# Stick-breaking attention: the suffix sums as fp32r products of high and low parts, one for every later key block, in place of fp32 products with a running total

## The chip, the cores and the metric

The kernel runs on one core of a Trainium2 chip. The metric is the device time of one execution in microseconds (us), the median of several runs. TensorE is PE in the profile (its weight loads PEld), VectorE is DVE, ScalarE is ACT, GpSimd is POOL, SyncE is SP and issues every DMA.

## The reference, cut to what matters

The program is a whole two-part transformer: two layers of differential and forgetting attention, a feed-forward block, a mixer with sparse attention and stick-breaking attention, a cross attention to a memory, and a second feed-forward block. The change touches the stick-breaking attention alone, with 8 heads of width 64 and T = 512 tokens:

```python
z = jnp.einsum('bhqd,bhkd->bhqk', qb, k).astype(jnp.float32) * scale
mask = kpos[None, :] < tq[:, None]
log_rem = jnp.where(mask, jax.nn.log_sigmoid(-z), 0.0)
suffix = lax.cumsum(log_rem, axis=3, reverse=True) - log_rem
a = jnp.where(mask, jnp.exp(jax.nn.log_sigmoid(z) + suffix), 0.0)
return jnp.einsum('bhqk,bhkd->bhqd', a, v).astype(q.dtype)
```

Since log_sigmoid(-z) is -softplus(z), and log_sigmoid(z) is z - softplus(z), the weight of a key is exp(z minus the sum of softplus over this key and all later ones that the query sees).

## The kernel before, in words

Five engines run their own instruction streams in order and meet at semaphores: `on.wait_ge(*sig[key])` waits for the instruction that incremented `sig` with that key. The stick-breaking stage is written by `sb_pe`, `sb_act`, `sb_dve` and `sb_pool`. It stands after the sparse attention and before the output projection of the mixer (`wout2`, in `memory_pe`).

The work is cut into 32 blocks, listed in `SB`: for each head a (0 to 7) the four key blocks j = 3, 2, 1, 0 of 128 keys. Keys lie on the partitions and queries on the columns. Key block j sees only queries from 128*j on, so its block is n = 512 - 128*j columns wide: 128, 256, 384 and 512. Block number k has one of six PSUM banks. `C("tri")` is a 128x128 matrix with -1 where the row is at or behind the column, `C("negone")` is all -1.

What happens to a block, in order:

1. PE, `begin(k)`: scores `ps<-QS,KS` (L2002, fp32), and the mask of the diagonal `ps<-strictR,identR` (L2004, fp32r, 128 columns).
2. DVE: max(z, 0) into `SPb` (L2070), then z - 2*max(z, 0), which is -|z|, into `Ab` (L2074).
3. ACT: Exp (L2040) and Ln of 1 + x (L2042), in place in `Ab`.
4. DVE: their sum, which is softplus, into `SPb` (L2081).
5. PE: `ps<-SPb,cst` (L2013, fp32) adds minus the sum within the key block to the scores. For j < 3, `ps<-RT,cst` (L2016, fp32) adds minus the sum over all later key blocks, from the running total `RT`.
6. DVE: adds the block to the running total (L2091, or L2095 and L2096).
7. ACT: the weights, Exp out of PSUM into `Ab` (L2046).
8. PE: behind the four blocks of a head the product with the values, `ps<-Ab,VSB` (L2030, fp32, four matmuls of 512 to 128 columns, x8 in the trace: an fp32 matmul is recorded as two).

The streams are skewed over one loop counter k: DVE and ACT do steps 2 and 3 of block k, DVE step 4 of block k-1, PE step 5 of block k-2 and then `begin(k + 2)`, ACT step 7 of block k-2, and PE step 8 of a head in the round in which k-3 is its last block. Behind each odd head ACT moves two heads' output out of PSUM into `fin` (named xb in the trace, L2053) and rounds it to fp32r (`xh`, L2056), and POOL subtracts to get the low part (`xl`, L2103). ACT issues both behind Exp and Ln of the next block but one and ahead of its next Exp. Nothing else is on POOL in this stage.

A "high and low" pair is how this program writes an fp32 number as two fp32r ones: high is the value rounded to fp32r, low is what is left. All weights and most activations are split so (L342 on ACT, L350 on POOL) and multiplied with fp32r matmuls.

Of the kernel before, what the change touches and what calls it, by code (L numbers as in the profile page):

```python
# [145 lines left out]
def program(nc, wstream, xT, memT, pos, const, param, out):  # L146
# [5 lines left out]
    with ctx:  # L152
# [103 lines left out]
        Pb2 = sb("Pb2", [128, 4, L], at=nsa)  # L256
        PT2 = [sb(f"PT2{i}", [128, 640], at=nsa) for i in range(2)]
        nsa.close()
        SPb = sb("SPb", [128, 2, 4, T], at=two)
        Ab = sb("Ab", [128, 2, 4, T], at=two)  # L260
        RT = sb("RT", [128, 2, T], at=two)
        two.close()
        mid.close()
        mem = ExitStack()
# [1727 lines left out]
        def sb_psum(a, j):  # L1992
            k = SB.index((a, j))
            return PS[:, 512 * sb_bank(k):512 * sb_bank(k) + T - 128 * j]

        def sb_pe(e, on):
            def begin(k):
                a, j = SB[k]
                q0 = 128 * j
                ps = claim(on, sb_bank(k), 1, prob["sb", a, j])  # L2000
                on.wait_ge(*v_out["ks", 3])
                e.matmul(ps[:, 0:T - q0], KS[:, a // 2, q0:q0 + 128], QS[:, a, q0:T], start=True, stop=False)  # L2002
                on.wait_ge(*a_one["strict"])
                e.matmul(ps[:, 0:128], identR[:, :], strictR, start=False, stop=True).then_inc(*score("sb", a, j))  # L2004
            begin(0)
            begin(1)
            for k in range(len(SB) + 3):
                if 2 <= k < len(SB) + 2:
                    a, j = SB[k - 2]
                    u, q0 = a % 2, 128 * j  # L2010
                    n, ps = T - q0, sb_psum(a, j)
                    on.wait_ge(*v_out["sb", "sp", a, j])
                    r = e.matmul(ps, C("tri"), SPb[:, u, j, 0:n], start=False, stop=True, skip_group_check=True)  # L2013
                    if j < 3:
                        on.wait_ge(*v_out["sb", "rt", a, j + 1])
                        r = e.matmul(ps[:, 128:n], C("negone"), RT[:, u, q0 + 128:T], start=False, stop=True,  # L2016
                                     skip_group_check=True)
                    r.then_inc(*one_mm("suffix", a, j))
                if k + 2 < len(SB):
                    begin(k + 2)  # L2020
                if k >= 3 and SB[k - 3][1] == 0:
                    a = SB[k - 3][0]
                    u, t_ = a % 2, a // 2
                    if u == 0:
                        claim(on, 6 + t_ % 2, 1, a_out["sb", "out", t_])
                    o = PS[:, 512 * (6 + t_ % 2):512 * (7 + t_ % 2)]
                    on.wait_ge(*prob["sb", a, 0])
                    for j in range(4):
                        vt = VSB[:, j, t_, 2 * u:2 * u + 2, :]
                        r = e.matmul(o[:, 128 * j:T], vt.rearrange("p a b -> p (a b)"), Ab[:, u, j, 0:T - 128 * j],  # L2030
                                     start=u == 0 and j == 0, stop=u == 1 and j == 3)
                    r.then_inc(*pv("sb", a))

        def sb_act(e, on):
            for k in range(len(SB) + 3):
                if k < len(SB):
                    a, j = SB[k]
                    e_ = Ab[:, a % 2, j, 0:T - 128 * j]
                    on.wait_ge(*v_out["sb", "arg", a, j])
                    e.activation(e_, e_, ACT.Exp).then_inc(*a_out("sb", "exp", a, j))  # L2040
                    on.wait_ge(*a_out["sb", "exp", a, j])
                    e.activation(e_, e_, ACT.Ln, bias=1.0).then_inc(*a_out("sb", "ln", a, j))  # L2042
                if 2 <= k < len(SB) + 2:
                    a, j = SB[k - 2]
                    on.wait_ge(*one_mm["suffix", a, j])
                    e.activation(Ab[:, a % 2, j, 0:T - 128 * j], sb_psum(a, j), ACT.Exp).then_inc(*prob("sb", a, j))  # L2046
                if k >= 3 and SB[k - 3][1] == 0 and SB[k - 3][0] % 2:
                    a = SB[k - 3][0]
                    t_ = a // 2
                    f, before = place(("sb", t_))  # L2050
                    on.wait_ge(*pv["sb", a])
                    on.wait_ge(*x_lo[("ao",) + before])
                    e.activation(fin[:, f, 0:T], PS[:, 512 * (6 + t_ % 2):512 * (7 + t_ % 2)], ACT.Copy).then_inc(  # L2053
                        *a_out("sb", "out", t_))
                    on.wait_ge(*a_out.now())
                    e.activation(xh[:, 4 + t_, M:L], fin[:, f, 0:T], ACT.Copy).then_inc(*x_hi("ao", "sb", t_))  # L2056

        def sb_dve(e, on):
            for k in range(len(SB) + 3):
                if k < len(SB):  # L2060
                    a, j = SB[k]
                    u, n = a % 2, T - 128 * j
                    o, sp = sb_psum(a, j), SPb[:, u, j, 0:n]
                    on.wait_ge(*score["sb", a, j])
                    if k == 0:
                        on.wait_ge(*turn["nsa1", 3])
                        on.wait_ge(*v_end["nsa1", 3, "gate"])
                    if a >= 2:
                        on.wait_ge(*one_mm["suffix", a - 2, 0])
                    e.tensor_scalar(sp, o, 0.0, None, ALU.max, ALU.bypass).then_inc(*v_out("sb", "max", a, j))  # L2070
                    on.wait_ge(*v_out.now())
                    if a >= 2:
# [3 lines left out]
                if 1 <= k < len(SB) + 1:  # L2076
                    a, j = SB[k - 1]
                    u, n = a % 2, T - 128 * j
                    sp = SPb[:, u, j, 0:n]
                    on.wait_ge(*a_out["sb", "ln", a, j])  # L2080
                    e.tensor_tensor(sp, sp, Ab[:, u, j, 0:n], ALU.add).then_inc(*v_out("sb", "sp", a, j))  # L2081
                if 2 <= k < len(SB) + 2:
                    a, j = SB[k - 2]
                    u, q0 = a % 2, 128 * j
                    n = T - q0
                    sp = SPb[:, u, j, 0:n]
                    on.wait_ge(*v_out["sb", "sp", a, j])
                    if j == 3:
                        if a >= 2:
                            on.wait_ge(*one_mm["suffix", a - 2, 0])  # L2090
                        e.tensor_copy(RT[:, u, 384:512], sp).then_inc(*v_out("sb", "rt", a, 3))  # L2091
                    elif j:
                        on.wait_ge(*one_mm["suffix", a, j])
                        on.wait_ge(*v_out["sb", "rt", a, j + 1])
                        e.tensor_copy(RT[:, u, q0:q0 + 128], sp[:, 0:128])  # L2095
                        e.tensor_tensor(RT[:, u, q0 + 128:T], RT[:, u, q0 + 128:T], sp[:, 128:n], ALU.add).then_inc(  # L2096
                            *v_out("sb", "rt", a, j))

        def sb_pool(e, on):
            for t_ in range(4):  # L2100
                f, _ = place(("sb", t_))
                on.wait_ge(*x_hi["ao", "sb", t_])
                e.tensor_tensor(xl[:, 4 + t_, M:L], fin[:, f, 0:T], xh[:, 4 + t_, M:L].bitcast(F32),  # L2103
                                ALU.subtract).then_inc(*x_lo("ao", "sb", t_))


        def mix_ao(k):
# [475 lines left out]
```

## Time and profile before

| | |
|---|---|
| median of 3 runs | 1977.92 us (1977.88 to 1987.02) |
| the profiled execution | 1985.47 us |
| its span | 1983.7 us |
| PE busy | 1921.9 us, 97% |
| PEld / DVE / ACT / POOL busy | 83% / 39% / 36% / 36% |
| chain that ended last, by engine | PE 88%, DVE 6%, ACT 3% |

The span is the stretch between the first and the last instruction in the trace. Busy shares are averages over stages with different limits. The chain that ended last is followed back from the last instruction, at each step to what released it.

### The profile page before, as it was taken

The numbers are of one execution on the slowest core, as the hardware profiler recorded it, in microseconds if no ns is written. First come the engines' busy times: TensorE is split into PE (matmuls) and PEld (weight loads), VectorE is DVE, ScalarE is ACT, GpSimd is POOL, SyncE is SP. The second block draws the span as 40 slices with busy tenths as digits, with TensorE's granted clock in tenths as the row PEclk, the third lists the DMA queues.
The fourth block names the chain that finished last, engine by engine and source line by source line (L and its number), as shares of the span: only waits on it lengthen the run. The fifth ranks groups of instructions, "written<-read, shape, count | busy, mean of one in ns | idle before, by whom it ended". The sixth has DMA issues, their size and how long they took to land.

```text
span 1983.7 us, 26722 instructions
## 1 busy us (share of the span) xinstructions
PE 1921.9 (97%) x10968; PEld 1646.1 (83%) x10968; DVE 779.8 (39%) x1308; ACT 707.4 (36%) x1328; POOL 712.1 (36%) x343
## 2 busy tenths in 40 slices
PE   7999989999998999999999999899999999999999
PEld 6999878989987897888888878799867878888887
DVE  5433373464326536441112255536676451111001
ACT  3112355321125544223222223435565552222211
POOL 4333201353331014555554423320003435555443
PEclk9999899999999999999999999979999999999999
DMA  4222200122221003222223233110002212222223
GB/s 142 86 79 82 65 1 1 54 85 86 78 85 41 1 13 100 87 94 96 96 91 98 92 109 118 65 43 2 1 1 97 95 54 96 96 96 96 91 88 108
DMA packets 40585, 144.22 MB, mean 73 GB/s; under 512 B 4624, under 2 KB 4880, under 8 KB 40336
## 3 DMA queue, kind: packets, MB, share of 16 engines
q1 hardware_dynamic: 40464, 142.51, 21.6%
q8 instruction: 87, 1.43, 0.3%
q14 instruction: 34, 0.28, 0.0%
HBM read 140.40 MB, written 2.10 MB: 72 GB/s over the span
## 4 chain that ended last, share of the span: by engine, by line
PE 88%; DVE 6%; ACT 3%; issue 1%; DMA 1%; POOL 0%; SPq 0%; DVEq 0%; ACTq 0%
PE ps L354 22%; PE ps L355 22%; PE ps L356 22%; PE ps L871 6%; PE ps L852 5%; PE ps L861 3%; PE ps L2030 1%; DMA raw<-wstream 1%; PE ps L2013 1%; DVE xl L425 1%; PE ps L2002 1%; PE ps L500 1%; PE ps L989 1%; ACT wh L342 1%; PE ps L1774 1%
## 5 line engine op out<-in xcount | busy, mean ns | idle before, releaser
L350 POOL TENSOR_TENSOR wl<-raw,wh 128x1024 fp32r<-128x1024 f32 (+2 forms) x254 | 603.6, 2376 | 838.9 <-ACT wh L342 838.9
L354 PE MATMUL ps<-xh,wh 128*128 128x512 f32 (+3 forms) x1752 | 626.4, 358 | 20.3 <-POOL wl L350 12.5
L355 PE MATMUL ps<-xl,wh 128*128 128x512 f32 (+3 forms) x1752 | 619.9, 354 | 0.0
L356 PE MATMUL ps<-xh,wl 128*128 128x512 f32 (+3 forms) x1752 | 618.1, 353 | 0.0
L342 ACT ACTIVATE wh<-raw 128x1024 fp32r<-128x1024 f32 (+2 forms) x254 | 266.0, 1047 | 969.8 <-PE ps L356 903.1
L354 PEld LDWEIGHTS ps<-xh,wh 128*128 128x128 f32 x1752 | 330.8, 189 | 75.4 <-issue 18.4
L355 PEld LDWEIGHTS ps<-xl,wh 128*128 128x128 f32 x1752 | 331.1, 189 | 49.0 <-issue 1.7
L356 PEld LDWEIGHTS ps<-xh,wl 128*128 128x128 f32 x1752 | 331.5, 189 | 47.2
L1116 POOL TENSOR_TENSOR xl<-xb,xh 128x512 fp32r<-128x512 f32 (+1 forms) x22 | 26.1, 1186 | 339.9 <-ACT xh L1025 339.9
L355 PE MATMUL ps<-aL,wh 128*128 128x512 f32 x352 | 139.4, 396 | 0.0
L356 PE MATMUL ps<-aH,wl 128*128 128x512 f32 x352 | 139.2, 396 | 0.0
L354 PE MATMUL ps<-aH,wh 128*128 128x512 f32 x352 | 139.2, 395 | 0.0
L910 DVE TENSOR_REDUCE nm<-ps 128x1 f32<-128x144 f32 (+7 forms) x208 | 99.6, 490 | 79.2 <-PE ps L852 78.6
L1409 DVE TENSOR_TENSOR tmpn<-xb,ps 128x512 f32<-128x512 f32 x44 | 30.3, 688 | 211.3 <-PE ps L356 208.6
L354 PE MATMUL ps<-wh,xh 128*128 128x256 f32 (+1 forms) x352 | 101.7, 289 | 5.8 <-DVE xb L1522 3.7
L897 ACT ACTIVATE PT<-ps 128x256 f32<-128x256 f32 (+4 forms) x142 | 70.6, 497 | 85.2 <-PE ps L861 79.7
L355 PE MATMUL ps<-wl,xh 128*128 128x256 f32 (+1 forms) x352 | 100.8, 286 | 0.0
L356 PE MATMUL ps<-wh,xl 128*128 128x256 f32 (+1 forms) x352 | 100.7, 286 | 0.0
L889 ACT ACTIVATE Pb<-ps,nm 128x256 f32<-128x256 f32 (+7 forms) x144 | 75.1, 523 | 31.4 <-DVE nm L910 30.6
L354 PEld LDWEIGHTS ps<-aH,wh 128*128 128x128 f32 x352 | 66.2, 188 | 16.1
L355 PEld LDWEIGHTS ps<-aL,wh 128*128 128x128 f32 x352 | 66.2, 188 | 16.0
L356 PEld LDWEIGHTS ps<-aH,wl 128*128 128x128 f32 x352 | 66.1, 188 | 15.9
(346 smaller groups left out, 2666.4 us busy)
## 6 DMA issues: line engine op xcount, KB each, us to landing
raw<-wstream SPq DMA_DIRECT2D x236, 512.0 KB, 3.5
raw<-wstream SPq DMA_DIRECT2D x16, 384.0 KB, 3.0
raw<-wstream SPq DMA_DIRECT2D x10, 528.0 KB, 3.6
h<-xT SPq DMA_DIRECT2D x4, 528.0 KB, 6.6
out<-h SPq DMA_DIRECT2D x8, 256.0 KB, 3.9
hm<-memT SPq DMA_DIRECT2D x1, 1024.0 KB, 4.8
cst<-const SPq DMA_DIRECT2D x1, 720.5 KB, 9.5
cst<-const SPq DMA_DIRECT2D x1, 320.0 KB, 4.0
```

What stands on the lines that cost most here:

```text
L342: e.activation(wh[p % 2][:, 0:n], raw[c % 2][:, 0:n], ACT.Copy).then_inc(*w_hi(p))
L350: e.tensor_tensor(wl[p % 2][:, 0:n], raw[c % 2][:, 0:n], wh[p % 2][:, 0:n].bitcast(F32), ALU.subtract).then_inc(*w_lo(p))
L354: e.matmul(o, w_h, x_h, start=start, stop=False)
L355: e.matmul(o, w_h, x_l, start=False, stop=False)
L356: return e.matmul(o, w_l, x_h, start=False, stop=stop)
L852: r = e.matmul(ps[:, x.o0 + lo:x.o0 + hi], lhsT, rhs, start=start, stop=stop)
L861: r = e.transpose(ps[0:b - a, 128 * j:128 * j + 128], plan.source(u)[:, a:b], ident)
L871: r = e.matmul(PS[:, lo + x.cols[0]:lo + x.cols[1]], buf[0:b - a, 128 * j:128 * j + 128], x.value(j, b - a), start=j == 0, stop=j == len(x ...
L889: e.activation(plan.slot(s)[:, 0:x.n], PS[:, lo:lo + x.n], ACT.Exp, bias=nm[:, s % 8:s % 8 + 1], accum_out=x.total[0]).then_inc(*prob(name ...
L897: e.activation(plan.PT[i % 2][:, 0:n], PS[:, lo:lo + n], ACT.Copy).then_inc(*a_flip(name, u))
L910: e.tensor_reduce(nm[:, u % 8:u % 8 + 1], PS[:, lo:lo + x.n], AX.X, ALU.max, negate=True).then_inc(*peak(name, u))
L1409: e.tensor_tensor(tmpn[:, f % 2, 0:T], xb[:, f % 2, 0:T], PS[:, 512 * b + 512:512 * b + 1024], ALU.mult).then_inc(*v_out(st, "gated", f))
```

## The change

The running total `RT` and its three DVE instructions (L2091, L2095, L2096 of before) go away, and so do both fp32 products of step 5. In their place each block's softplus, now kept in `Ab`, is rounded to fp32r into `SPh` (ACT for j = 3 and 2, a DVE cast for j = 1 and 0), and POOL subtracts to get the low part `SPl`. PE multiplies both parts with `negR` for every later key block of the head (0, 1, 2 or 3 of them), and with `triR` for the block itself. `SPb` shrinks to two buffers that hold max(z, 0) only. POOL's output subtractions are put between its new ones: behind the low part of block j = 2 of heads 2, 4 and 6, and one at the end. Two small ACT instructions make `triR` and `negR` at the start of the stage.

```diff
         def sb_pe(e, on):
...
-                    on.wait_ge(*v_out["sb", "sp", a, j])
-                    r = e.matmul(ps, C("tri"), SPb[:, u, j, 0:n], start=False, stop=True, skip_group_check=True)
-                    if j < 3:
-                        on.wait_ge(*v_out["sb", "rt", a, j + 1])
-                        r = e.matmul(ps[:, 128:n], C("negone"), RT[:, u, q0 + 128:T], start=False, stop=True,
+                    on.wait_ge(*a_one["tri"])
+                    for i in range(3, j, -1):
+                        for part in (SPh, SPl):
+                            e.matmul(ps[:, 128 * (i - j):n], negR, part[:, u, i, 0:T - 128 * i], start=False, stop=True,
                                      skip_group_check=True)
+                    for part, done in ((SPh, sb_high(a, j)), (SPl, x_lo["sb", "sp", a, j])):
+                        on.wait_ge(*done)
+                        r = e.matmul(ps, triR, part[:, u, j, 0:n], start=False, stop=True, skip_group_check=True)
                     r.then_inc(*one_mm("suffix", a, j))
...
         def sb_act(e, on):
+            e.activation(triR, C("tri"), ACT.Copy)
+            e.activation(negR, C("negone"), ACT.Copy).then_inc(*a_one("tri"))
...
+                if 1 <= k < len(SB) + 1 and SB[k - 1][1] > 1:
+                    a, j = SB[k - 1]
+                    on.wait_ge(*v_out["sb", "sp", a, j])
+                    sb_low_free(on, a, j)
+                    e.activation(SPh[:, a % 2, j, 0:T - 128 * j], Ab[:, a % 2, j, 0:T - 128 * j], ACT.Copy).then_inc(
+                        *x_hi("sb", "high", a, j))
...
         def sb_dve(e, on):
...
-                    sp = SPb[:, u, j, 0:n]
+                    t = Ab[:, u, j, 0:n]
                     on.wait_ge(*a_out["sb", "ln", a, j])
-                    e.tensor_tensor(sp, sp, Ab[:, u, j, 0:n], ALU.add).then_inc(*v_out("sb", "sp", a, j))
-                if 2 <= k < len(SB) + 2:
...
-                        e.tensor_copy(RT[:, u, q0:q0 + 128], sp[:, 0:128])
-                        e.tensor_tensor(RT[:, u, q0 + 128:T], RT[:, u, q0 + 128:T], sp[:, 128:n], ALU.add).then_inc(
-                            *v_out("sb", "rt", a, j))
+                    e.tensor_tensor(t, SPb[:, (k - 1) % 2, 0:n], t, ALU.add).then_inc(*v_out("sb", "sp", a, j))
+                    if j <= 1:
+                        on.wait_ge(*v_out.now())
+                        sb_low_free(on, a, j)
+                        e.tensor_copy(SPh[:, u, j, 0:n], t).then_inc(*v_out("sb", "high", a, j))
 
         def sb_pool(e, on):
...
+            for k, (a, j) in enumerate(SB):
+                u, n = a % 2, T - 128 * j
+                sb_low_free(on, a, j)
+                on.wait_ge(*sb_high(a, j))
+                e.tensor_tensor(SPl[:, u, j, 0:n], Ab[:, u, j, 0:n], SPh[:, u, j, 0:n].bitcast(F32),
+                                ALU.subtract).then_inc(*x_lo("sb", "sp", a, j))
+                if j == 2 and a in (2, 4, 6):
+                    outputs(a // 2 - 1)
+            outputs(3)
```

Three places show how the instructions stand. The first is PE in a head's last round, before: the sums of block j = 0, the scores of a block of the next head, and the sums of that head's block j = 3.

```order
L2013 MATMUL ps<-SPb,cst 128x512
L2016 MATMUL ps<-RT,cst 128x384
L2002 MATMUL ps<-QS,KS 128x512
L2004 MATMUL ps<-strictR,identR 128x128
L2013 MATMUL ps<-SPb,cst 128x128
L2002 MATMUL ps<-QS,KS 128x128
```

The same place after the change:

```order
L2026 MATMUL ps<-SPh,negR 128x128
L2026 MATMUL ps<-SPl,negR 128x128
L2026 MATMUL ps<-SPh,negR 128x256
L2026 MATMUL ps<-SPl,negR 128x256
L2026 MATMUL ps<-SPh,negR 128x384
L2026 MATMUL ps<-SPl,negR 128x384
L2030 MATMUL ps<-SPh,triR 128x512
L2030 MATMUL ps<-SPl,triR 128x512
L2013 MATMUL ps<-QS,KS 128x512
L2015 MATMUL ps<-strictR,identR 128x128
L2030 MATMUL ps<-SPh,triR 128x128
L2030 MATMUL ps<-SPl,triR 128x128
```

L2026 are the products with `negR`, L2030 those with `triR`; each fp32 product over a running total has become up to six fp32r ones of 128, 256 and 384 columns, and only the last `triR` product needs the newest low part.

The second place is DVE, over two rounds in which a new head begins, before:

```order
L2081 TENSOR_TENSOR SPb<-SPb,Ab 128x384
L2095 COPY RT<-SPb 128x128
L2096 TENSOR_TENSOR RT<-RT,SPb 128x128
L2070 TENSOR_SCALAR SPb<-ps 128x128
L2074 SCALAR_TENSOR_TENSOR Ab<-SPb,ps 128x128
L2081 TENSOR_TENSOR SPb<-SPb,Ab 128x512
L2095 COPY RT<-SPb 128x128
```

and after, from the same point on (the sum of the previous head's block j = 1 is the first row of each):

```order
L2102 TENSOR_TENSOR Ab<-SPb,Ab 128x384
L2106 CAST SPh<-Ab 128x384
L2091 TENSOR_SCALAR SPb<-ps 128x128
L2095 SCALAR_TENSOR_TENSOR Ab<-SPb,ps 128x128
L2102 TENSOR_TENSOR Ab<-SPb,Ab 128x512
L2106 CAST SPh<-Ab 128x512
L2091 TENSOR_SCALAR SPb<-ps 128x256
```

L2102 is the softplus sum, now with both inputs and the output in SBUF as before; the running total's two instructions behind it are gone, and a cast (L2106) of the same width stands there.

The third place is POOL, before: the splits of the mixer's last weights, the low parts of the sparse attention's output, the four low parts of this stage's output, and the splits for the output projection.

```order
L350 TENSOR_TENSOR wl<-raw,wh 128x1056 x6
L350 TENSOR_TENSOR wl<-raw,wh 128x1024 x6
L1116 TENSOR_TENSOR xl<-xb,xh 128x4x128 x4
L2103 TENSOR_TENSOR xl<-xb,xh 128x512 x4
L350 TENSOR_TENSOR wl<-raw,wh 128x1024 x14
L1116 TENSOR_TENSOR aml<-xb,amh 128x2x128 x4
```

and after, in the middle of the stage (the end of head 1, head 2 and its successor):

```order
L2118 TENSOR_TENSOR SPl<-Ab,SPh 128x512
L2118 TENSOR_TENSOR SPl<-Ab,SPh 128x128
L2118 TENSOR_TENSOR SPl<-Ab,SPh 128x256
L2112 TENSOR_TENSOR xl<-xb,xh 128x512
L2118 TENSOR_TENSOR SPl<-Ab,SPh 128x384
L2118 TENSOR_TENSOR SPl<-Ab,SPh 128x512
L2118 TENSOR_TENSOR SPl<-Ab,SPh 128x128
```

The output's low part (L2112) now stands between the low parts of two blocks (L2118) of one head, and what comes behind it on POOL waits for it.

## Rows read from the trace of the kernel before

**Rows 1.** Windows view: us, busy PE, PEld, DVE, ACT, POOL, granted clock, DMA
```profile
...
1320.00:1335.00 15.00, 15.00 (x78) 15.00 (x77) 6.71 (x25) 6.17 (x27) 0.00 (x0) 0.50 0.00 0
...
1428.00:1497.00 69.00, 66.93 (x266) 43.51 (x265) 51.36 (x137) 44.67 (x103) 5.08 (x4) 0.99 0.00 1
...
```

**Rows 2.** Chain of waits in order of time, the stick-breaking stage: start, us, what
```profile
...
1447.29 2.22 PE ps L2030 x8
...
1449.53 0.61 ACT xb L2053
...
1450.16 0.63 ACT xh L2056
1450.79 0.53 ACT Ab L2040
...
1451.34 0.64 ACT Ab L2042
...
1452.00 0.70 DVE SPb L2081
...
1452.75 1.13 PE ps L2013 x2
...
1456.00 2.21 PE ps L2030 x8
...
1464.22 2.22 PE ps L2030 x8
...
1498.40 0.23 PE ps L354
...
```

**Rows 3.** Chain of waits from 1456.00 to 1464.22 (8.22 us), by line
```profile
...
by line: PE ps L2030 32.7%; PE ps L2013 28.2%; PE ps L2002 26.3%; PE ps L2016 15.8%; PE ps L2004 2.9%
...
```

**Rows 4.** Groups of instructions, 1428 to 1497
```profile
...
L2081 DVE TENSOR_TENSOR SPb<-SPb,Ab 128x128 f32<-128x128 f32 (+3 forms) x32 | 15.7, 491 | 2.6 <-ACT Ab L2042 2.6
L2074 DVE SCALAR_TENSOR_TENSOR Ab<-SPb,ps 128x128 f32<-128x128 f32 (+3 forms) x32 | 15.6, 487 | 1.1
L2070 DVE TENSOR_SCALAR SPb<-ps 128x128 f32<-128x128 f32 (+3 forms) x32 | 15.5, 486 | 0.6 <-PE ps L2004 0.2
...
```

**Rows 5.** Timeline of PE: fp32r matmuls of 264 columns, back to back
```profile
...
1290.02 0.28 PE L354 MATMUL ps<-wh,xh 128*128 128x264 f32 x1
1290.14 0.28 PE L355 MATMUL ps<-wl,xh 128*128 128x264 f32 x1
...
```

**Rows 6.** Timeline of PE in the sparse attention: 128 and 64 columns
```profile
...
1395.89 0.61 PE L861 MATMUL ps<-identR,Pb 128*128 128x128 f32 x4
1396.25 0.70 PE L852 MATMUL ps<-KSW,QN 128*128 128x512 f32 x2
1396.79 0.22 PE L852 MATMUL ps<-maskR,identR 128*128 128x128 f32 x1
1396.85 1.05 PE L871 MATMUL ps<-VSW,PT 128*128 128x64 f32 x8
1397.73 0.50 PE L861 MATMUL ps<-identR,Pb 128*128 128x128 f32 x3
```

**Rows 7.** Groups by form, POOL
```profile
...
L2103 POOL TENSOR_TENSOR xl<-xb,xh 128x512 fp32r<-128x512 f32 x4 | 5.1, 1276 | 65.6 <-ACT xh L2056 65.6
...
L1116 POOL TENSOR_TENSOR aml<-xb,amh 128x256 fp32r<-128x256 f32 x4 | 2.9, 728 | 16.2 <-ACT amh L1025 16.2
...
```

**Rows 8.** Groups by form, DVE copies from SBUF to SBUF
```profile
...
L2236 DVE COPY QM<-xb 64x512 f32<-64x512 f32 x4 | 1.7, 421 | 0.1
...
L2226 DVE COPY KM<-xb 128x256 f32<-128x256 f32 x2 | 0.6, 294 | 0.1
...
```

**Rows 9.** Timeline, 444 to 448: POOL and DVE side by side
```profile
...
444.12 2.40 POOL L350 TENSOR_TENSOR wl<-raw,wh 128x1024 fp32r<-128x1024 f32 x1 [3.61 <-ACT wh L342]
...
444.35 2.72 DVE L513 TENSOR_TENSOR scratch<-xb,cst 128x512 f32<-128x512 f32 x1
...
447.10 0.69 DVE L515 TENSOR_TENSOR scratch<-ps,cst 128x512 f32<-128x512 f32 x1
...
```

More of the change, by code:

```diff
@@ L258, in program @@
         nsa.close()
-        SPb = sb("SPb", [128, 2, 4, T], at=two)
+        SPb = sb("SPb", [128, 2, T], at=two)
         Ab = sb("Ab", [128, 2, 4, T], at=two)
-        RT = sb("RT", [128, 2, T], at=two)
+        SPh = sb("SPh", [128, 2, 4, T], F32R, at=two)
+        SPl = sb("SPl", [128, 2, 4, T], F32R, at=two)
+        triR, negR = (sb(n, [128, 128], F32R, at=two)[:, :] for n in ("triR", "negR"))
         two.close()
@@ L1994, in sb_psum, with sb_high, sb_low_free @@
             return PS[:, 512 * sb_bank(k):512 * sb_bank(k) + T - 128 * j]
+        def sb_high(a, j):
+            return (x_hi if j > 1 else v_out)["sb", "high", a, j]
+        def sb_low_free(on, a, j):
+            if a >= 2:
+                on.wait_ge(*one_mm["suffix", a - 2, 0])
         def sb_pe(e, on):
@@ L2062, in sb_dve @@
                     u, n = a % 2, T - 128 * j
-                    o, sp = sb_psum(a, j), SPb[:, u, j, 0:n]
+                    o, sp = sb_psum(a, j), SPb[:, k % 2, 0:n]
                     on.wait_ge(*score["sb", a, j])
@@ L2078, in sb_dve, with outputs @@
                     u, n = a % 2, T - 128 * j
-                    sp = SPb[:, u, j, 0:n]
+                    t = Ab[:, u, j, 0:n]
                     on.wait_ge(*a_out["sb", "ln", a, j])
-                    e.tensor_tensor(sp, sp, Ab[:, u, j, 0:n], ALU.add).then_inc(*v_out("sb", "sp", a, j))
-                if 2 <= k < len(SB) + 2:
[L2083 to L2094, printed above, removed]
-                        e.tensor_copy(RT[:, u, q0:q0 + 128], sp[:, 0:128])
-                        e.tensor_tensor(RT[:, u, q0 + 128:T], RT[:, u, q0 + 128:T], sp[:, 128:n], ALU.add).then_inc(
-                            *v_out("sb", "rt", a, j))
+                    e.tensor_tensor(t, SPb[:, (k - 1) % 2, 0:n], t, ALU.add).then_inc(*v_out("sb", "sp", a, j))
[3 more added lines that the diff above has]
+                        e.tensor_copy(SPh[:, u, j, 0:n], t).then_inc(*v_out("sb", "high", a, j))
         def sb_pool(e, on):
-            for t_ in range(4):
+            def outputs(t_):
                 f, _ = place(("sb", t_))
```

4 lines of the change are left out of this document (2 added, 2 removed).

## The prediction

> **What bounds the kernel now.** I read the windows view of the stage first. From 1428 to 1497 PE is busy 66.93 of 69.00 us, at a granted clock of 0.99; DVE has 51.36, ACT 44.67 and POOL 5.08 [rows 1]. So PE paces the stage, and POOL is nearly free. The chain of waits tells how evenly. The product with the values (L2030) begins at 1447.29, 1456.00 and 1464.22 [rows 2]. A head therefore takes 8.71 us or 8.22 us in turn, 16.93 us for two. The 8.22 us are PE work without a gap: the chain by line names PE alone [rows 3]. The 8.71 us hold a detour: L2030 ends, ACT moves the output out (L2053) and rounds it (L2056), only then does Exp and Ln of the next head's 512-column block (L2040, L2042), DVE adds (L2081), and PE, which has meanwhile run out of other work, begins L2013 at 1452.75 [rows 2]. The reader is to keep this detour in mind: the change puts two more instructions behind its last step.
>
> **What the change removes on PE.** In the head of 8.22 us, L2013 has 28.2% and L2016 15.8% [rows 3], which is 2.32 + 1.30 = 3.62 us a head.
>
> **What it adds on PE.** 20 fp32r matmuls a head: two of 512 columns, four of 384, six of 256, eight of 128. 512 columns take 0.23 (L354 at 1498.40) [rows 2]; 264 columns take 0.12 back to back [rows 5], which I use for 256; 384 lies between, 0.18. For 128 columns the trace gives two ends. The fp32r mask product takes 0.06 (1396.79 to 1396.85), with its weights loaded under a longer matmul. Eight of only 64 columns take 0.88, 0.11 each, and there the loads must set the pace. Four of 128 columns in a row take 0.36, 0.09 each [rows 6]. The new ones also come in rows, so I take 0.09. Sum: 0.46 + 0.72 + 0.72 + 0.72 = 2.62 us (2.4 to 2.8). PE saves 1.0 us a head (0.8 to 1.2), and its own work falls from 8.22 to 7.2. If nothing else came in, the stage would lose 8 us.
>
> **What it adds beside PE.** DVE loses the running total and gains casts of 384 and 512 columns. I price them as copies in SBUF: 421 ns for 512 columns, 294 for 256, so about 0.36 for 384 [rows 8]. ACT gains two roundings of the narrow blocks a head, each under the 0.63 of the 512-column one (L2056 to L2040) [rows 2], so its 44.67 us of 69 [rows 1] stay under 55. POOL gains one subtraction a block: 1276 ns for 512 columns and 728 for 256 give 2.14 ns a column, so 1.00 for 384 and 0.45 for 128 [rows 7]; 3.46 us a head, 28 us in all, where it did almost nothing. By busy time it all fits. By latency it doesn't: before, PE could begin a block's own sum as soon as DVE had added (L2081); now a cast (0.42) and a subtraction (1.28) come between, for the widest block.
>
> **DVE and POOL get in each other's way.** At 444.12 POOL begins a subtraction of 2.40 us. DVE begins at 444.35 a tensor_tensor with both inputs in SBUF and takes 2.72 us, where the one at 447.10 with an input in PSUM takes 0.69 [rows 9]. The first ends 0.55 us after POOL's end (447.07 against 446.52). So a DVE addition of two SBUF tensors waits for a POOL subtraction that runs. L2081 is such an addition, and POOL now subtracts in this stage. L2070 and L2074 read PSUM and pass.
> The Trainium skill ("SBUF — State Buffer", Who interferes with whom) has this as a rule: with two SBUF inputs against a GpSimd instruction that reads SBUF, the second one to issue is blocked until the first finishes. Read literally, the blocked addition would cost its full 0.69 behind POOL's end and not the 0.55 of the row; with five blocked ones in two heads that would be 0.14 x 5 x 4 = 2.8 us more than my sum. The row has a duration, so I use the row.
>
> **The even head (a new pair begins), walked through.** From one L2030 to the next: L2030 and hand-over 2.24; ACT move 0.63 and rounding 0.63 (1449.53 to 1450.79) [rows 2]; POOL's low part of the output 1.28, which now stands ahead of the low part of block j = 1, 1.00 [rows 7]; DVE's sum of block j = 0, which arrives while that runs and ends 0.55 behind it [rows 9]; cast 0.42 [rows 8]; low part 1.28 [rows 7]; then PE's last triR product 0.23, the scores of the next block but one and its mask 0.86 + 0.06, two 128-column products 0.18, and a narrow score and mask 0.28: 1.61. (0.86 is four passes' worth of 512 fp32 columns, as in L2030, whose 512, 384, 256 and 128 columns take 2.21 together [rows 2]: 2.21 x 512/1280 = 0.88.) Sum: 2.24 + 1.26 + 2.28 + 0.55 + 0.42 + 1.28 + 1.61 = 9.64, and four hand-overs of 0.02 to 0.05 more: 9.8 us, against 8.71.
>
> **The odd head.** PE needs 7.2. DVE: L2070, L2074 and L2081 have 15.5 + 15.6 + 15.7 = 46.8 us for 8 heads [rows 4], 5.85 a head, with the casts 6.6. On top L2081 waits: the 1.28 of the low part of block j = 0 runs while DVE does its two operations on the next 256 columns (0.84), 0.44 too long; the 1.00 of block j = 1 against two on 128 columns (0.57), 0.43; the 0.73 of block j = 2, which starts late since ACT rounds it, about 0.4. Together 7.9; neighbouring DVE operations overlap a little, so I take 7.8, against 8.22. In the odd head DVE takes PE's place as the bound, and 0.4 of the 1.0 us saved is left.
>
> **The ends.** The first and the last head have no other head's work to cover the longer way. Behind the last sum stood fp32 products of 512 and 384 columns (at the 2.21 us for 1280 columns of L2030, 0.88 + 0.66); now cast and subtraction 1.70 and one product of 0.23: 0.4 more, and one or two port waits of 0.4: 1.2 at either end. The two ACT instructions for `triR` and `negR` lie where ACT waits for the sparse attention's last output: nothing; without that cover at most 2 x 0.63.
>
> **Sum.** A pair: 9.8 + 7.8 = 17.6 against 16.93, +0.7; four pairs +2.7; ends +2.4. Together +5 us on the profiled execution (1985.47 to about 1990.5). The rest of the program isn't touched. The three runs before lie at 1977.88, 1977.92 and 1987.02, so the profiled one is of the upper kind; on the median I forecast 1977.9 + 5 = 1983. A difference under 0.5% (9.9 us) can hardly be told from no change here, given that spread.
>
> **Rivals.**
> *PE's saving comes through* (10%). Speaks for it: PE is the bound today, and POOL's subtractions could hide in the three rounds between a block's scores and its sums. Against it: the detour already costs 0.49 us where nothing was added behind it. Time: 1977.9 - 8 = 1970; with 0.06 for each 128-column matmul 1968, which is just 0.5%.
> *The ports don't clash here* (15%): POOL's short subtractions slip in beside DVE's PSUM work. Then the odd head falls to PE's 7.2 and the even one still has the added cast and subtraction, less 0.5: 9.3. A pair is 16.5, the ends cost 0.8: -1.7 + 1.6, no change, 1978.
> *Slower by over 0.5%* (14%): TensorE is granted the lower of its two levels. From 1320 to 1335 the clock is 0.50 (1.2 GHz) with PE busy throughout, on 78 matmuls [rows 1]. The change makes this stage one of narrow matmuls with gaps. At half rate PE's 14.4 us of work in a pair of 17.6 becomes 28.8, so a low stretch of L us costs 0.39 L. It decides from 13 us on; 15 us as in the row cost 6, on top of the 5: 1989.
> *POOL waits for DVE as DVE does for POOL* (10%): the trace shows one direction only [rows 9]. Six POOL instructions of a pair are on the walked way (three in each head); if each meets half of a DVE sum (0.49) [rows 4], that is 0.25 x 6 x 4 = 6 us more: 1989, at the bound.
> *My forecast* (51%): 1979 to 1987 as its own range.
>
> **Numbers.** The range must take in the case without clashes and most of the slow one: 1974 to 1992, which leaves out the saving that comes through and a long low stretch. Faster by over 0.5%: 4%, only the far end of the first rival. Slower: 18%, over half of the two rivals at 1989 and a tail of my own case. The rest, 78%, within 0.5%.
>
> **What the profile would show.** Starts of the value product 7.8 and 9.8 us apart in turn. PE waiting for POOL's low parts in the waits view, above all before triR products of 512 columns, some 0.5 us each. The sum of DVE (L2102) at a mean well above 0.49, since it waits for the port. Fp32r 128-column products 0.09 apart. Wrong if POOL isn't in the chain, if the mean of DVE's sum stays at 491 ns, or if the clock in the stage falls below 0.95.

## The result, and the profile after

The changed kernel takes 1985.18 us (median of 22 runs, 1981.69 to 1994.07) against 1978.87 us for the kernel before on the same chip. The ratio is 1.0027, with an interval of 1.0016 to 1.0038: 5.3 us slower (the medians lie 6.3 apart), inside the half per cent. Two runs of before, at 3154 and 6661 us, are of a slower state and stay out of the ratio.

| | before | after |
|---|---|---|
| span of the profiled execution | 1983.7 us | 1987.3 us |
| PE busy | 1921.9 us | 1914.4 us |
| DVE / ACT / POOL busy | 779.8 / 707.4 / 712.1 us | 789.1 / 711.7 / 741.5 us |
| first score load to the start of the last value matmul | 1427.2 to 1498.1: 70.9 us | 1423.2 to 1501.7: 78.5 us |

The two spans should not be subtracted as they stand. The profiled execution of before has a stretch at half clock in the sparse attention (0.50 from 1320 to 1335 [rows 1]); that of after has 1.00 there. The stage itself can be compared. It is 7.6 us longer in this execution.

The chain of waits after the change, two heads of it (start, us, what), answers to [rows 2] and [rows 3]:

```profile
...
1458.10 0.17 PE ps L2026 x2
1458.28 0.29 PE ps L2030 x2
...
1459.06 0.51 PE ps L2026 x4
1459.57 0.35 PE ps L2030 x2
...
1460.62 0.86 PE ps L2026 x6
1461.49 0.46 PE ps L2030 x2
...
1462.87 0.23 PE ps L2030 x2
...
1463.42 2.22 PE ps L2043 x8
...
1465.67 0.61 ACT xb L2074
...
1466.30 0.64 ACT xh L2077
...
1467.01 1.27 POOL xl L2112
1468.28 1.42 POOL SPl L2118
...
1469.74 0.44 PE ps L2030
...
1473.69 2.21 PE ps L2043 x8
...
```

L2043 is the value product, once L2030. The odd head runs from 1455.89 to 1463.42 in 7.53 us on PE alone. Its lines L2026 (negR) and L2030 (triR) are the 20 new matmuls: 0.17 + 0.29 + 0.51 + 0.35 + 0.86 + 0.46 + 0.23 = 2.87 us, where 3.62 stood. The even head takes 10.27 us, from 1463.42 to 1473.69. It runs over the output's move (L2074) and rounding (L2077) to POOL: the output's low part (L2112), the low part of block j = 1 (L2118), and at 1469.74 back to PE. From there to the next value product, 3.95 us, PE works without another wait.

The waits view of the stage says the same from the side of PE, and shows what POOL waits for:

```profile
...
POOL SPl L2118 <- ACT SPh L2062: 20.1, 13, 3.2
...
PEld ps L2030 <- POOL SPl L2118: 11.8, 9, 2.7
...
POOL SPl L2118 <- DVE SPh L2106: 11.1, 13, 1.1
PE ps L2030 <- POOL SPl L2118: 9.0, 6, 2.5
...
```

PE and its weight loads wait for POOL's low parts, up to 2.7 us at a time. The three long waits of PE, 2.47 to 2.48 us each, are all before the `triR` product of block j = 1 (384 columns) in heads 2, 4 and 6; the one wait before a product of 512 columns is 0.85 us, in head 7. The groups of the stage (mean ns behind the busy time) answer to [rows 4]:

```profile
...
L2118 POOL TENSOR_TENSOR SPl<-Ab,SPh 128x256 fp32r<-128x256 f32 (+3 forms) x31 | 28.7, 924 | 32.6 <-ACT SPh L2062 20.1 <-DVE SPh L2106 11.1 <-PE ps L2030 1.3
L2102 DVE TENSOR_TENSOR Ab<-SPb,Ab 128x384 f32<-128x384 f32 (+3 forms) x30 | 22.8, 761 | 6.0 <-ACT Ab L2057 6.0
...
L2106 DVE CAST SPh<-Ab 128x384 fp32r<-128x384 f32 (+1 forms) x16 | 8.3, 520 | 0.5
...
```

L2102 is the addition that had a mean of 491 ns as L2081 [rows 4]; it does the same work and now has 761. The cast has 520 ns. The timeline inside the even head's gap shows both directions of the waiting:

```profile
...
1467.01 1.27 POOL L2112 TENSOR_TENSOR xl<-xb,xh 128x512 fp32r<-128x512 f32 x1 [2.13 <-ACT xh L2077]
...
1468.14 0.69 DVE L2102 TENSOR_TENSOR Ab<-SPb,Ab 128x512 f32<-128x512 f32 x1 [1.93 <-ACT Ab L2057]
1468.23 1.46 POOL L2118 TENSOR_TENSOR SPl<-Ab,SPh 128x384 fp32r<-128x384 f32 x1
...
1468.87 1.10 DVE L2106 CAST SPh<-Ab 128x512 fp32r<-128x512 f32 x1
...
1469.74 0.44 PE L2030 MATMUL ps<-SPl,triR 128*128 128x384 f32 x1 [2.48 <-POOL SPl L2118]
...
1470.05 1.28 POOL L2118 TENSOR_TENSOR SPl<-Ab,SPh 128x512 fp32r<-128x512 f32 x1 [0.36 <-DVE SPh L2106]
...
1471.83 0.39 PE L2030 MATMUL ps<-SPl,triR 128*128 128x512 f32 x1
...
```

DVE's addition begins at 1468.14. POOL's subtraction of 384 columns begins 0.09 later and takes 1.46 us, where 1.01 is its usual time. DVE's cast begins at 1468.87, meets that subtraction and takes 1.10, where 0.43 is usual. The low part of block j = 0 is ready at 1471.33, half a microsecond before its product (1471.83).

The last view is the windows of the stage, with the columns of [rows 1]:

```profile
...
1445.00:1450.00 5.00, 2.88 (x18) 2.28 (x16) 3.10 (x7) 3.16 (x7) 3.01 (x3) 1.00 0.00 0
1450.00:1455.00 5.00, 4.66 (x15) 3.63 (x15) 3.48 (x7) 2.21 (x6) 2.02 (x3) 0.66 0.00 0
1465.00:1470.00 5.00, 2.52 (x17) 2.16 (x17) 2.97 (x7) 3.15 (x7) 2.68 (x2) 1.00 0.00 0
1485.00:1490.00 5.00, 2.53 (x11) 2.17 (x11) 3.82 (x7) 3.21 (x9) 3.96 (x4) 0.86 0.00 0
1490.00:1495.00 5.00, 5.00 (x19) 3.26 (x18) 3.09 (x6) 2.92 (x7) 1.05 (x3) 0.80 0.00 0
1428.00:1497.00 69.00, 60.01 (x296) 45.19 (x295) 56.48 (x104) 46.55 (x112) 31.07 (x33) 0.95 0.00 1
...
```

The granted clock is 0.66 behind the gap at 1445 to 1450, and 0.86 and 0.80 around that of 1485 to 1495. Behind the equal gap of 1465 to 1470 it stays at 1.00. Over the stage (1428 to 1497) it is 0.95, where before had 0.99 [rows 1].

The timed runs are recorded with their mean granted clock too. Its mean is 0.9914 over the 22 runs of the changed kernel, and 0.9931 to 0.9934 over those of the kernel before in the three sessions of experiments below (without one run of 3156 us). Between the changed kernel's own runs, 1981.69 us at 0.995 and 1994.07 at 0.985, a thousandth of clock goes with about 1.2 us. So about 2 of the 5.3 us are the clock's; this is an estimate, across sessions.

### The profile page after: what moved, and what is told of

Same layout as the page of the kernel before. It is cut to its first block, busy times and chain, and to the rows that moved or that the text cites. A ratio compares the mean times of both kernels' runs of the same rounds, so it can differ in the third digit from the quotient of the medians.

```text
span 1987.3 us, 26867 instructions
## 1 busy us (share of the span) xinstructions
PE 1914.4 (96%) x11016; PEld 1643.1 (83%) x11016; DVE 789.1 (40%) x1284; ACT 711.7 (36%) x1346; POOL 741.5 (37%) x375
## 4 chain that ended last, share of the span: by engine, by line
PE 86%; DVE 7%; ACT 3%; DMA 1%; issue 1%; POOL 1%; SPq 0%; DVEq 0%; ACTq 0%
PE ps L356 22%; PE ps L357 22%; PE ps L358 22%; PE ps L873 5%; PE ps L854 5%; PE ps L863 3%; DMA raw<-wstream 1%; ACT wh L344 1%; PE ps L2043 1%; DVE xl L427 1%; PE ps L502 1%; PE ps L991 1%; POOL wl L352 1%; PE ps L2013 1%; PE ps L410 0%
## 5 line engine op out<-in xcount | busy, mean ns | idle before, releaser
L899 ACT ACTIVATE PT<-ps 128x256 f32<-128x256 f32 (+4 forms) x142 | 70.6, 497 | 79.7 <-PE ps L863 74.6
```

Of the source, the lines that this page charges most:

```text
L899: e.activation(plan.PT[i % 2][:, 0:n], PS[:, lo:lo + n], ACT.Copy).then_inc(*a_flip(name, u))
```

## The experiments

All are timed in 5 rounds against the kernel before on the same chip; the ratio is to that kernel. This table gives the time from one value product's start to the next in each profiled execution, by the timeline. Heads 1, 3 and 5 are odd, 2, 4 and 6 even. The stage is counted from the first score load to the start of the last value matmul. The last row's kernel was timed twice.

| kernel | ratio (interval) | heads 1, 3, 5 | heads 2, 4, 6 | head 7 | stage |
|---|---|---|---|---|---|
| before | 1 | 8.22, 8.22, 8.22 | 8.72, 8.71, 8.43 | 6.56 | 70.9 |
| changed | 1.0027 (1.0016 to 1.0038) | 7.90, 7.53, 7.56 | 11.86, 10.27, 11.53 | 6.96 | 78.5 |
| outputs behind j = 0 | 1.0030 (1.0015 to 1.0046) | 7.92, 7.52, 7.54 | 9.64, 9.65, 9.30 | 7.21 | 73.7 |
| outputs in POOL's gap | 1.0036 (1.0024 to 1.0048) | 7.89, 8.50, 8.50 | 9.26, 9.25, 8.92 | 8.39 | 77.7 |
| POOL writes only | 1.0005 (0.9988 to 1.0022) | 7.53, 7.52, 7.53 | 9.80, 9.80, 9.46 | 6.47 | 72.3 |
| no low parts | 0.9977 (0.9961 to 0.9993) | 7.53, 7.53, 7.53 | 8.59, 8.59, 8.55 | 5.63 | 67.4 |
| own blocks in fp32 | 1.0019 (1.0004 to 1.0035) | 8.42, 8.41, 8.42 | 9.73, 9.73, 9.44 | 6.43 | 74.6 |
| filler in the gap | 1.0018 (1.0008 to 1.0029) | 7.89, 7.57, 7.56 | 10.28, 10.28, 9.93 | 7.27 | 75.7 |
| output later | 1.0027 (1.0013 to 1.0041) | 7.89, 8.47, 8.47 | 7.90, 7.89, 7.56 | 8.43 | 73.7 |
| output later, POOL writes only | 0.9976 (0.9966 to 0.9986) | 7.53, 7.52, 7.52 | 7.53, 7.53, 7.20 | 6.47 | 65.4 |
| before, output later | 1.0004 (0.9994 to 1.0014) | 8.23, 8.24, 8.25 | 8.67, 8.68, 8.67 | 6.63 | 70.9 |
| block j = 0 in fp32, output early | 1.0009 (0.9993 to 1.0025) | 7.92, 7.92, 7.92 | 8.82, 8.81, 8.48 | 6.63 | 71.7 |
| block j = 0 in fp32, output later | 0.9991 (0.9982 to 0.9999), 0.9989 (0.9980 to 0.9998) | 7.92, 7.92, 7.92 | 7.92, 7.92, 7.58 | 6.48 | 68.6 |

**The outputs behind block j = 0.**

```diff
-                if j == 2 and a in (2, 4, 6):
+                if j == 0 and a in (2, 4, 6):
                     outputs(a // 2 - 1)
```

> The changed kernel, with POOL's low part of the output moved from between the low parts of blocks j = 2 and j = 1 of heads 2, 4 and 6 to behind that of block j = 0. Theory (in the even head the whole chain runs through POOL: output 1.27, then the low parts): each of the three even heads loses that 1.27, PE waits about 3.8 us less in all, 1981.5 us. Rival (the even head waits for DVE's sums or for the clock, POOL's place in it is by chance): within 1 us of the changed kernel, 1985.

Half of it came. The even heads fell from 10.27 to 9.64, not by 1.27, and the ratio, 1.0030, can't be told from the changed kernel's. The chain, and two rows of PE's timeline, say why:

```profile
...
1464.17 0.44 DVE SPh L2106
...
1464.68 1.27 POOL SPl L2118
1465.95 0.58 POOL xl L2112
1466.54 0.66 issue
1467.20 0.47 POOL SPl L2118
...
1467.71 0.33 PE ps L2030
...
1468.37 2.21 PE ps L2043 x8
...
```

```profile
...
1466.01 0.50 PE L2030 MATMUL ps<-SPl,triR 128*128 128x512 f32 x1 [0.86 <-POOL SPl L2118]
...
1467.71 0.33 PE L2030 MATMUL ps<-SPl,triR 128*128 128x128 f32 x1 [0.17 <-POOL SPl L2118]
...
```

With the output's low part out of the way, the path over ACT's Exp and Ln, DVE's sum and cast and the low part of block j = 0 is the long one. PE waits 0.86 us for that low part, and 0.17 for the next head's block j = 3, before which the output's low part now stands; the single wait of 2.48 us is gone. So POOL's place in the chain is shown, and a second path of nearly the same length stands behind it. In this profiled execution the stage is 2.8 us longer than before, in the medians the kernel is 5.2 us slower; the mean clock of its runs, 0.9912 against 0.9931, would account for about 2 of the difference.

**No low parts.** POOL's 32 subtractions are left out and PE multiplies the high part twice, so the sums lack the low parts.

```diff
-                        for part in (SPh, SPl):
+                        for part in (SPh, SPh):
...
-                    for part, done in ((SPh, sb_high(a, j)), (SPl, x_lo["sb", "sp", a, j])):
+                    for part, done in ((SPh, sb_high(a, j)), (SPh, sb_high(a, j))):
```

> The changed kernel without POOL's subtractions: PE multiplies the high part twice in their place, so the sums lose their low parts, and PE has the same 20 fp32r products a head. Theory (PE's saving is real and is lost behind POOL): PE is the bound again, value products 7.3 to 7.5 us apart, 1971 to 1972 us, 7 under the kernel before. Rival (128-column fp32r products in rows save nothing over fp32 ones): about 1979, as before.

PE's saving is real: odd heads of 7.53 us, and 0.9977, some 4.5 us where 7 was expected. The rival is out. But the even heads take 8.59, not 7.5: their chain runs over the output's move and rounding, Exp, Ln, DVE's sum and cast, and on to the rounding on ACT of the next head's block j = 3. POOL costs at most the rest of 10.27.

**POOL writes only.** Each subtraction is a memset of equal length, which reads nothing; the low parts are left out as above.

```diff
-                e.tensor_tensor(SPl[:, u, j, 0:n], Ab[:, u, j, 0:n], SPh[:, u, j, 0:n].bitcast(F32),
-                                ALU.subtract).then_inc(*x_lo("sb", "sp", a, j))
+                if k >= 2:
+                    on.wait_ge(*x_lo[("sb", "sp") + SB[k - 2]])
+                flat = SPl[:, k % 2, :, :].rearrange("p a b -> p (a b)")
+                e.memset(flat[:, 0:{128: 429, 256: 754, 384: 1077, 512: 1402}[n]].bitcast(F32), 0.0).then_inc(
+                    *x_lo("sb", "sp", a, j))
```

> The changed kernel with each subtraction of POOL replaced by a fill of the low-part buffer that is sized to take as long (0.455, 0.73, 1.0, 1.27 us) and reads nothing; PE multiplies the high part twice, so the low parts are left out. It keeps POOL's latency and takes away the meeting of two readers. Theory with the port as a term of its own: L2102's mean falls from 761 ns to about 490, odd heads fall to 7.3 us, even ones to about 9, total 1979 to 1980. Rival (only the latency of cast and subtraction matters, the port nothing): 1985.

The groups of its stage:

```profile
...
L2121 POOL MEMSET SPl<- 128x1402 f32 (+3 forms) x29 | 25.4, 877 | 24.5 <-ACT SPh L2062 13.1 <-DVE SPh L2106 7.4 <-issue 4.0
...
L2102 DVE TENSOR_TENSOR Ab<-SPb,Ab 128x256 f32<-128x256 f32 (+3 forms) x27 | 13.3, 493 | 6.8 <-ACT Ab L2057 6.8
...
```

And DVE's cast beside one of the fills, in an even head:

```profile
...
1442.41 1.00 POOL L2121 MEMSET SPl<- 128x1077 f32 x1
...
1443.06 0.63 DVE L2106 CAST SPh<-Ab 128x512 fp32r<-128x512 f32 x1
...
```

POOL's instructions have a mean of 877 ns, near the 924 of the changed kernel's subtractions, and DVE's addition is back at 493 ns. The stage loses 6.2 us of 78.5, of which some 3 are the clock (below). The port is a term of its own. The total is the expected one, the heads are not: the even ones are still at 9.80, 0.47 under 10.27, which is what POOL's subtraction of 384 columns had lost behind DVE's addition. The rest is latency: the output's move and rounding, its low part and the low part of j = 1. The fills do not free the cast: in the three even heads it starts while a fill runs and takes 0.62 to 0.63 us for 0.43.

**Own blocks in fp32.** The product with `tri` is done in fp32 on `Ab`, as before; the pairs serve later key blocks only, and block j = 0 isn't split.

```diff
+                    if j < 3:
+                        on.wait_ge(*x_lo["sb", "sp", a, j + 1])
...
-                        r = e.matmul(ps, triR, part[:, u, j, 0:n], start=False, stop=True, skip_group_check=True)
+                    on.wait_ge(*v_out["sb", "sp", a, j])
+                    r = e.matmul(ps, C("tri"), Ab[:, u, j, 0:n], start=False, stop=True, skip_group_check=True)
...
```

> The changed kernel with the sum within a key block done in fp32 from the softplus itself, as before; only the products for later key blocks use the high and low parts, which nobody needs before the next block, and block j = 0 isn't split at all. PE's work a head: 8.2 less 1.30 of the running-total products plus 1.4 for the 12 fp32r ones, 8.3. Theory (the cost is the split in the way of the own block): about the time before, 1978 to 1981. Rival (POOL's and DVE's load on the ports slows the stage wherever the split stands): 1984 or more.

1.0019 (1981.83 us against 1977.63), a little over the theory's range. The odd heads, 8.41, are PE work and dearer than before (8.22): the twelve products for later blocks cost more than the three over a running total. The even ones stay at 9.73, since the output still stands ahead of the low part of j = 1, which block j = 0 needs.

**The outputs in POOL's gap**, behind the low part of block j = 3 of heads 3, 5 and 7.

> The changed kernel, with POOL's low part of the output behind the low part of block j = 3 of heads 3, 5 and 7, where POOL next waits 1.8 to 3.2 us for a rounding. Theory (with the outputs behind block j = 0 they stood in the way again, ahead of the low part of the next head's block j = 3, and PE still waited): even heads fall from 9.64 there to 9.0 or less, ratio to the kernel before 1.001 to 1.002. Rival (the even head is held by the chain of ACT and DVE behind the output's move and rounding, not by POOL): as with the outputs behind j = 0, 1.003.

Not as expected: 1.0036. The even heads fell to 9.25, but the odd ones rose to 8.50, so a pair took 17.75 against 17.80, and against 17.17 with the outputs behind j = 0. The even head's chain runs over ACT's Exp and Ln of the 512-column block and then over DVE, as the rival said; then DVE's addition of 256 columns stands beside the output's subtraction (1.27 us from 1448.32) and takes 1.34 us for 0.42, and DVE stays the chain into the odd head. So the place is worth 0.6 us a pair, and no place of these three is free. The end of the stage ran at clocks of 0.64 and 0.68, and head 7 took 8.39.

**The output later**: in addition ACT's move and rounding come one round later, behind Exp and Ln of the next 512-column block.

```diff
-                if k >= 3 and SB[k - 3][1] == 0 and SB[k - 3][0] % 2:
-                    a = SB[k - 3][0]
+                if k >= 4 and SB[k - 4][1] == 0 and SB[k - 4][0] % 2:
+                    a = SB[k - 4][0]
```

> The same, and ACT moves and rounds the output one round later, behind Exp and Ln of the 512-column block and not ahead of them. Theory (the detour over the output is what the low parts lengthen): even heads fall to about 7.6 to 8.0, PE is the bound in most heads, and PE's saving shows: ratio 0.997 to 0.9985, 1972 to 1975. Rival (POOL's and DVE's waits for each other hold every head): 1.000 to 1.002.

The even heads did what was expected (7.90), the ratio did not: 1.0027. Its profiled execution had a low stretch in the sparse attention, so the stage counts: 73.7 us, 2.8 more than before. Heads 1 to 6 together are 2.3 us shorter than before; the start is 1.2 longer, head 7 1.9, and the last value product, at a clock of 0.55 from 1500 on, takes 4.6 us for 2.4. The chain from 1450 to 1475, by line, and the group of DVE's addition:

```profile
...
by line: DVE Ab L2102 44.3%; DVE SPb L2091 22.9%; DVE Ab L2095 17.8%; issue 11.6%; DVE SPh L2106 7.1%; DVEq L142 0.5%
...
```

```profile
...
L2102 DVE TENSOR_TENSOR Ab<-SPb,Ab 128x128 f32<-128x128 f32 (+3 forms) x32 | 27.5, 859 | 0.5 <-ACT Ab L2057 0.5
...
```

DVE alone is the bound, at 7.9 us a head and 8.47 where POOL's output falls in, and its additions take 859 ns each. So the rival names the right cause in the middle heads, though 1.0027 is over its range too, and the next run tests it.

**The output later, POOL writes only.**

> The kernel with the later output, whose chain of waits is DVE alone (7.89 and 8.47 us a head), with POOL's subtractions replaced by fills of equal length that read nothing; PE multiplies the high part twice, so the low parts are left out. Theory (DVE is the bound there only because its sums wait for POOL's reads): both heads fall to PE's 7.5, the mean of L2102 to 0.49, ratio 0.996 to 0.997. Rival (DVE is too slow without POOL too): 7.8 or more a head.

```profile
...
L2102 DVE TENSOR_TENSOR Ab<-SPb,Ab 128x256 f32<-128x256 f32 (+3 forms) x27 | 13.3, 493 | 1.6 <-ACT Ab L2057 1.6
...
```

Heads 1 to 5 fall to PE's 7.53, the addition to 493 ns, the ratio to 0.9976, a little over the expected 0.996 to 0.997. DVE's own work isn't the bound; its waits for POOL's reads are. 859 - 493 = 0.37 us for each of four additions a head.

**The kernel before, output later.** The same edit of ACT on the kernel before.

> The kernel before, with the same later place of the output's move and rounding on ACT, nothing else. Theory: the 0.49 us of the three even heads go, 1.5 us, ratio 0.9992; the rest of the kernel before is PE work. If it were 0.997 or less, the later place alone and not PE's saving would explain what the previous kernel gains.

Not as expected: 0.9992 lies just outside the interval around 1.0004, and the even heads stay at 8.67. Their chain has another link now, and the timeline shows what stood beside it:

```profile
...
1438.87 0.45 PE ps L2016 x2
...
1439.34 1.34 DVE RT L2095
1440.68 0.34 DVE RT L2096
...
1441.07 0.91 PE ps L2016 x2
...
```

```profile
...
1437.72 0.23 DVE L2095 COPY RT<-SPb 128x128 f32<-128x128 f32 x1 [1.54 <-PE ps L2016]
...
1439.33 1.27 POOL L2103 TENSOR_TENSOR xl<-xb,xh 128x512 fp32r<-128x512 f32 x1 [21.33 <-ACT xh L2056]
1439.34 1.34 DVE L2095 COPY RT<-SPb 128x128 f32<-128x128 f32 x1
...
```

The copy of 128 columns into the running total (L2095) takes 1.34 us and holds PE back. Elsewhere it takes 0.23, also where DVE has first waited 1.54 us for PE's product over the total. It takes 1.34 three times, once in each even head, and each time POOL's subtraction for the output (L2103, 1.27 us) began 0.01 us before it; the copy ends 0.08 us behind POOL's end. In its new place the output's subtraction meets this copy. So the detour over the output is gone here, and a wait of DVE for POOL has come in its stead. That the even heads would fall to the odd ones' 8.24 without it is likely, but no run shows it.

**Block j = 0 in fp32, output later, and output early.** Block j = 0 has no later key block, so its pair serves only its own sum. Here that sum is an fp32 product, and the widest cast and subtraction go.

```diff
+                    if j == 0:
+                        on.wait_ge(*v_out["sb", "sp", a, 0])
+                        r = e.matmul(ps, C("tri"), Ab[:, u, 0, 0:n], start=False, stop=True, skip_group_check=True)
-                    for part, done in ((SPh, sb_high(a, j)), (SPl, x_lo["sb", "sp", a, j])):
+                    for part, done in ((SPh, sb_high(a, j)), (SPl, x_lo["sb", "sp", a, j])) if j else ():
```

> As the kernel with the later output, but the own sum of block j = 0 is done in fp32 from the softplus itself, so the 512-column cast and subtraction, which no later block needs, go. PE's work a head 7.5 + 0.4 = 7.9. Theory: no POOL or DVE step of 512 columns is left in the way, the ends of the stage lose their extra 1.2 us each, ratio 0.997 to 0.998. Rival (PE's work alone counts): slower than the kernel with the later output by 0.4 x 8 = 3 us.

> The kernel with the own sum of block j = 0 in fp32, with ACT's move and rounding of the output back ahead of Exp and Ln. Theory: the detour ends in DVE's sum as in the kernel before, and the even heads take 8.4 to 8.7 us against 7.92; ratio 1.0000 to 1.0005. Rival (the fp32 own sum alone makes the gain): ratio 0.999, as with the later output.

> The kernel with the own sum of block j = 0 in fp32 and the later output once more, beside the other three. Expected 0.9985 to 0.9995, heads of 7.92 us.

With the output later the kernel is faster than the kernel before: 0.9991 and 0.9989 in two sessions, some 2 us, with intervals that end at 0.9999 and 0.9998. Less than the expected 0.997 to 0.998, since the stage, 68.6 us against 70.9, had no more than 2.3 us to give. One head from value product to value product, by line of the chain:

```profile
...
by line: PE ps L2046 27.9%; PE ps L2013 27.9%; PE ps L2026 19.6%; PE ps L2033 10.8%; PE ps L2030 10.8%; PE ps L2015 3.8%
...
```

Nothing but PE is left in it, at 7.92 us, the 7.5 + 0.4 of the expectation. With the output early the even heads take 8.8 and the gain is gone (1.0009, an interval across 1). The intervals of the two kernels overlap a little; that the place of the output matters is shown by the heads.

**Filler in the gap.** Two fp32 products that nobody reads, put before PE's wait for the low part of j = 1 of heads 2, 4 and 6.

```diff
+                        if j == 1 and a in (2, 4, 6) and part is SPl:
+                            on.wait_ge(*a_out["sb", "out", a // 2 - 1])
+                            b = 6 + (a // 2 - 1) % 2
+                            for _ in range(2):
+                                e.matmul(PS[:, 512 * b:512 * b + 512], KS[:, 0, 0:128], QS[:, 0, :], start=True, stop=True,
+                                         skip_group_check=True)
                         on.wait_ge(*done)
```

> The changed kernel, with two fp32 products of 512 columns (1.7 us) into the unused output bank in the 2.4 us for which PE waits for the low part of block j = 1 of heads 2, 4 and 6; nobody reads them. Theory (in the profile of the changed kernel the granted clock fell to 0.66 and 0.80 after two of these gaps, and these even heads took 11.9 and 11.5 us where the one at full clock took 10.27): all even heads take about 10.3, ratio 1.001 to 1.002. Rival (the falls are rare in other executions and don't bear on the median): ratio 1.0027 as without them.

The even heads take 10.28, 10.28 and 9.93 and the granted clock stays at 1.00 in the stage from 1425 on. Against 11.86, 10.27 and 11.53 that is 3.2 us in the profiled execution. The ratio is 1.0018, under 1.0027, but the two intervals overlap. The mean clock of its runs is 0.9940 against 0.9914 for the changed kernel, and none of them is under 0.992. That agrees with some 2 us of the median for the clock.

## Why the prediction was right, point by point

**The size.** 1983 was forecast, 5 us over the median then known; 5.3 us by the ratio was measured. In part that is luck. The sum takes four pairs, but only three even heads (2, 4 and 6) stand behind an output: three at +1.09 and four odd ones at -0.42 are +1.6, not +2.7, and with the ends 4.0. At full clock the profiled stage is 4.4 us longer, with even heads dearer and odd heads cheaper than forecast, and the clock, which is in no term, brought more.

**PE's work.** The new matmuls cost 2.87 us a head, not 2.62. Two of 128 columns take 0.17 once a head and 0.22 to 0.23 otherwise, where 0.18 was priced; two of 256 take 0.29, not 0.24. 384 and 512 columns were priced right. PE's floor is 7.53, not 7.2.

**The even head.** Forecast 9.8, measured 10.27 at full clock. The links up to PE's restart were named rightly: move, rounding, output's low part, low part of j = 1. In the step "DVE's sum of block j = 0, which arrives while that runs and ends 0.55 behind it" the order was wrong: the sum began 0.09 before POOL's subtraction of j = 1, and POOL waited, 1.46 for 1.00. That is the rival in which POOL waits for DVE too, with its price at one of six places. Behind that the forecast's path was wrong: it goes on over DVE's sum, the cast and the low part of j = 0, 0.55 + 0.42 + 1.28 and then 1.61 on PE, 3.86 us. In the trace PE restarts at 1469.74, works 3.95 us on its own and doesn't wait for that low part. That the two are almost equally long is luck. For the same reason the sign "above all before triR products of 512 columns, some 0.5 us each" failed: the waits are 2.5 us before those of 384 columns. In the run with the outputs behind j = 0 the sum, the cast and that low part are in the chain.

**The odd head.** Forecast 7.8 with DVE as the bound, measured 7.53 to 7.56 with PE as the bound. The step "in the odd head DVE takes PE's place" failed for heads 3 and 5: in the 2.5 us that PE loses in an even head DVE catches up. Head 1, which has no such gap ahead of it, takes 7.90 on a chain of DVE up to 1440.64, as forecast. Its own pace was sized well: with the output later, when PE no longer idles, the heads without POOL's output take 7.89 on a chain of DVE.

**The ends.** From the first score load to the first value product 12.8 us against 11.7: 1.1 more, forecast 1.2. At head 7 only 0.4 more, forecast 1.2.

**The port.** That DVE's addition waits for POOL's reads was read from one place [rows 9] and holds: 491 to 761 ns, and 493 with a POOL that only writes. The two operations on PSUM pass, as forecast (the row for it, at 447.10, stood where POOL was idle and couldn't show it): 692 and 687 ns for 512 columns (L2091, L2095) against 687 and 688 before. The step prices the waits of the addition alone; the casts wait as well, 1.10 for 0.43 in each of the three even heads, and their mean is 520 ns where 0.36 and 0.42 were priced. The Trainium skill ("SBUF — State Buffer", Who interferes with whom) gives the same condition, two SBUF inputs against a GpSimd instruction that reads, and for the addition the memset run agrees with it. Its words let the blocked instruction follow the first in full; the rows give less, 0.55 us behind POOL's end for a 0.69 us addition, and, for POOL behind DVE's end at 1468.83, 0.86 us of a 1.00 us subtraction.

**The clock.** It was priced as a rival at 14% and left out of the sum. Over the stage it stood at 0.95, just at the forecast's own sign of being wrong. In the profiled execution it fell twice for a short time at PE's gaps and made two even heads 1.6 us longer each (11.86 against 10.27, and head 6 11.53 against the 9.93 of the filler's run).

In the stage of that execution: three even heads at full clock 1.5 to 1.6 more each (4.6), odd heads 0.3, 0.7 and 0.7 less, head 7 0.4 and the start 1.1 more, the clock about 3.2: 7.6, as measured.

## What to carry to other kernels

A saving on the bounding engine is worth only what the next link lets through: here PE got 0.7 us a head cheaper, and a cast and a subtraction in the way of its last product took it back. Splitting an operand pays where somebody later needs the parts; the one block whose pair served only its own product is 0.4 us a head dearer on PE in fp32, and the stage is still shorter with it, since a cast and a subtraction of 512 columns go. Before work is put on idle POOL, look at what DVE does at that moment: an addition of two SBUF tensors, a cast or a copy in SBUF and a subtraction on POOL take turns. With the later output 32 short subtractions made DVE the bound of the heads: it was busy 15.06 of 15.79 us, while the same instructions beside fills take 12.35 of 15.05. A single subtraction that starts just before a short copy can do it too, as the kernel before with the later output shows.

## What the runs showed of the hardware that was not expected

The waiting at the port goes both ways, by who begins first: 1.46 for 1.00 us on POOL, 1.10 for 0.43 us on a DVE cast, 1.34 for 0.23 us on a DVE copy of 128 columns. For the addition it doesn't appear when POOL only writes (493 ns); for the cast, which has one input in SBUF, it does (0.63 for 0.43).

The granted clock can fall inside a stage in which PE has gaps of 2.5 us, and need not: behind three like gaps of one execution it fell twice. Over many runs the mean clock is 0.9914 for the changed kernel with its gaps, and 0.9940 with the gaps filled. A low clock also explains the spread of this program's runs at least in part: the profiled executions of before and of the kernel with the later output, with spans of 1983.7 and 1989.7, have a clock of 0.50 for 15 us or more from 1320 on; the other profiled executions do not.

An edit can take one wait away and make another of the same size. In the kernel before, the detour over the output gave even heads of 8.72 us. With the output later they take 8.67, with a DVE copy in the chain that POOL's subtraction holds up, and the edit measured as nothing.
